# A two-block transformer kernel: FFN panel splits moved behind the tile work, keys copied by DMA, banks and table reads reordered

## The chip, the core and the metric

The kernel runs on one core of one Trainium2 chip. The metric is the time of one execution on the device, in microseconds. TensorE is PE (its weight loads are PEld), VectorE is DVE, ScalarE is ACT, GpSimd is POOL, and SyncE is SP, which issues nearly all DMAs.

## The reference

A sequence of 256 tokens, width 1024, fp32, runs through two blocks. Block 1 has two layers: a gated unit (gMLP) and then a convolutional FFN; differential attention with a relative bias and then a second such FFN. Block 2: a SwiGLU FFN, a mixer of latent attention (MLA) and block attention (MoBA) with positions, a second SwiGLU FFN, and a last norm.

```python
def conv_ffn(x, w_up, conv_w, conv_b, w_down):          # D_FF = 2816
    h = causal_dwconv(x @ w_up, conv_w, conv_b)
    g, u = h[..., :D_FF], h[..., D_FF:]
    return (jax.nn.gelu(g) * u) @ w_down
def swiglu(x, w_gate, w_up, w_down):
    return (jax.nn.silu(x @ w_gate) * (x @ w_up)) @ w_down
...
z = jax.nn.gelu(x @ w_in); u, v = z[..., :W], z[..., W:]   # gMLP
v = einsum('gpq,bnqgc->bnpgc', ws, layernorm(v)) + b_s
return (u * v) @ w_out
...
bias = rel_bias[t5_bucket(kpos - qpos)]                    # diff_attention, added to the scores
...
q, k = [q_nope, apply_rope(q_rope)], [k_nope, apply_rope(k_rope)]   # mla_attention
```

## The kernel before

All weights lie in HBM as 352 panels of 128x1024 fp32 (512 KB). Each goes the same way. SP loads panel n into `raw`, a ring of five buffers (`load(n)`, which waits until DVE has finished panel n-5). ACT copies it to `w_high` in the short format of TensorE (L441), and DVE subtracts to get `w_low` (L853); both are rings of eight. PE multiplies each product in three parts (high by high, high by low, low by high). Queues are written out by hand: each engine runs its list in order, and waits on semaphores. `upto(n)` on ACT and on DVE is a call that splits all panels up to n at this place of the list, so how far the splits run ahead is a matter of where these calls stand.

The stages by panel number: GMLP (24 panels), FFN0 (66), DIFF (32), FFN1 (66), FFN2 (66), MIX (32), FFN3 (66). In an FFN the hidden width is cut in 22 tiles f. Tiles 0 and 1 come from the first four panels of the stage (`first_four`, `first_two`, `turn_first`); for f from 2 on PE makes gate and up products (g, u: L1404 and L1408), and from f = 4 on also the down product (d) of tile f-4 (L1462). The last six down panels are in `tail`, which also begins the next stage. For a tile of a convolutional FFN the work goes: ACT copies the low product out (`lows_out`, L528), DVE adds it (`summed`, L957), ACT does the last tap (`last_tap`, L556), DVE the other taps (`first_taps`, L984), ACT the gelu (L562), DVE the product (`gated_up`, L993), ACT the high part (`hidden_high`, L532), DVE the low part (`hidden_low`, L966). Between them stand calls of `share(f, base, left)`, which spread the splits of the panels that have room in the ring. PE starts g of tile 4 only when `summed` of tile 2 is done, since both use one pair of PSUM banks, and d of tile f only after `hidden_low(f)`.

At a stage boundary b (`boundary(b)`) y is added to h, h is normed, and PE turns the parts (`turn_x`, L1470) and starts the value products (L1439 to L1445). In GMLP a product with ones spreads the first rms over partitions (`r0`), another gives row sums; both go to banks of Y, as do the eight u tiles (`tile_out`, L1389 to L1391). In MIX, `krt` holds the rotated shared key, which goes to all eight heads of `kT` (POOL, L426); `column_factors` on PE gives the factors of queries and keys, `CR` and `rkv`, and `cb_r` tells that both are read. The table `rel_rows` of the bias is written to HBM, and read back in eight DMAs `table_rows(a)` into `bias`, which POOL finishes (`bias_r`).

Of the kernel before, what the change touches and what calls it, by code (L numbers as in the profile page):

```python
# [91 lines left out]
def build_program(nc, io):  # L92
    with ExitStack() as ctx:
# [29 lines left out]
        CRs, rkvs = sb("cr", [P, T]), sb("rkv", [P, T])  # L123
# [3 lines left out]
        diag = sb("diag", [P, TT, P])  # L127
# [19 lines left out]
        lamrow = sb("lamrow", [P, 4, DIFF_D])  # L147
        posi = sb("posi", [P, T + TT], I32)
        posb = sb("posb", [P, 2, T + TT], I32)
# [8 lines left out]
        posf = w3[:, 0, 0:3 * (T + TT)].rearrange("p (a b) -> p a b", a=3)  # L158
        vg = big1[:].rearrange("p (t c) -> p t c", t=TT)
# [17 lines left out]
        CR, rkv = CRs[:], rkvs[:]  # L177
# [127 lines left out]
        def _(sp):  # L305
# [46 lines left out]
            for n in range(10, PANELS):  # L352
# [4 lines left out]
                if n == FFN0 + 2:  # L357
                    sp.wait_ge(vp_r, 2)
                    sp.wait_ge(rel_wr, 16)
                    sp.dma_start(lamrow[:].rearrange("p a b -> p (a b)"),  # L360
                                 io["lam"].to_broadcast([P, 4 * DIFF_D])).then_inc(lam_in, 16)
                if n >= FFN0 + 6 and (n - FFN0 - 6) % 4 == 0 and n < FFN0 + 6 + 32:
                    table_rows((n - FFN0 - 6) // 4)
# [9 lines left out]
        def _(pool):  # L373
# [30 lines left out]
            for q, c0, n in ((0, 0, P), (1, P, T)):  # L404
# [26 lines left out]
        def _(act):  # L431
# [88 lines left out]
            def share(f, base, left):  # L520

                seen = base + (FFN_AT["u", f] if f >= 2 else 4)
# [11 lines left out]
            def ffn(ph, base, with_conv):  # L534
                upto(base + 4)
                first_two(ph, base)
                if with_conv:
                    conv_ffn(ph, base)
                else:
                    swiglu_ffn(ph, base)  # L540
                preload(ACT.Sqrt)
                upto(base + 3 * NF + 1)

            def conv_ffn(ph, base):
# [19 lines left out]
                for f in range(NF):  # L564
# [4 lines left out]
                    if f < NF - 1:  # L569
                        share(f, base, 3)  # L570
# [192 lines left out]
            upto(DIFF + 34)  # L763
# [80 lines left out]
        def _(dve):  # L844
# [55 lines left out]
            def boundary(b):  # L900

                base = STARTS[b]
                if b in POST:
# [5 lines left out]
                    upto(base + (3 if b in (1, 3) else 2))  # L909
# [38 lines left out]
            def share(f, base, left):  # L948
                seen = base + (FFN_AT["u", f] if f >= 2 else 4)
                todo = min(seen + RING - (f < NF - 2), PANELS - 1) + 1 - made[0]  # L950
# [26 lines left out]
            def conv_ffn(ph, base):  # L977
# [18 lines left out]
                for f in range(NF):  # L996
# [5 lines left out]
                    if f < NF - 1:  # L1002
# [6 lines left out]
                upto(base + 3 * NF)  # L1009
# [82 lines left out]
            v.tensor_scalar(posb[:, 0, :], posi[:], 12, None, ALU.arith_shift_right)  # L1092
            link(v.tensor_scalar(posb[:, 1, :], posi[:], 4095, None, ALU.bitwise_and))
            v.tensor_copy(posf[:, 0, :], posi[:])
            v.tensor_copy(posf[:, 1:3, :], posb[:]).then_inc(pos_r, 1)
            upto(10)
            for t in range(TT):
# [5 lines left out]
                if t == 0:  # L1103
                    dve.wait_ge(r0_ps, 1)
                    v.tensor_copy(rkvs[:], Y[:, 2, 0:T]).then_inc(r0_r, 1)
# [6 lines left out]
            for k in range(KT):  # L1112
                r = Y[:, k // 4, (k % 4) * P:(k % 4 + 1) * P]
# [10 lines left out]
            U_BANK = (2, 0, 1, 3)  # L1124
# [130 lines left out]
            upto(DIFF + 34)  # L1255
# [40 lines left out]
            upto(B + 16)  # L1296
# [3 lines left out]
            dve.wait_ge(cb_r, 1)  # L1300
            weigh(8)
# [79 lines left out]
        def _(pe):  # L1381
# [235 lines left out]
            pe.wait_ge(ws_masked, 1)  # L1617
            for c in range(2):
                last = mm(Y[:, c, :], ones[:], wsT[:, half(c)], start=True, stop=True)
            last.then_inc(rowsum_r, 1)  # L1620
            pe.wait_ge(r0_r, 1)
            for k in range(KT):
                if k == 2:
                    pe.wait_ge(off_r, 1)
# [8 lines left out]
                tile_out(GMLP + 8 + k, Y[:, (2, 0, 1, 3)[k // 2], (k % 2) * T:(k % 2 + 1) * T])  # L1633
# [4 lines left out]
            pe.wait_ge(u_r, 3)  # L1638
# [192 lines left out]
            pe.wait_ge(kt_rot, 1)  # L1831
# [163 lines left out]
```

## Time and profile before

| | before |
|---|---|
| median of 3 runs | 1089.14 us (1087.27 to 1092.41) |
| the profiled execution, its own time | 1089.01 us |
| its span in the trace | 1087.2 us |
| PE busy | 97% of the span |
| DVE busy | 72% |
| ACT busy | 60% |
| mean granted TensorE clock | 0.997 of full speed |

The busy shares are means over all stages. The time is bounded by PE wherever PE has no idle time; the places where it has some, and who ended it, are what the views below are read for.

### The profile page before, as it was taken

How to read it: one execution, taken by the hardware profiler on the slowest of the kernel's cores; microseconds unless marked ns; L12 is line 12 of the kernel's file. 1: busy time of each engine (PE TensorE's matmuls, PEld its weight loads, DVE VectorE, ACT ScalarE, POOL GpSimd, SP SyncE). 2: the span in 40 equal slices, each digit the busy share in tenths (PEclk: the TensorE clock that was granted, in tenths of full speed). 3: DMA queues.
4: the chain of work that ended last, by engine and by line, in shares of the span. 5: the costliest groups of instructions: out<-in, count | busy, mean ns of one | idle time of the engine just before them, and what ended most of it. 6: DMA issues, size and time to landing. Idle time of an engine off the chain costs nothing.

```text
span 1087.2 us, 15597 instructions
## 1 busy us (share of the span) xinstructions
PE 1057.9 (97%) x5944; PEld 912.6 (84%) x5944; DVE 777.7 (72%) x1229; ACT 654.2 (60%) x1176; POOL 38.4 (4%) x39
## 2 busy tenths in 40 slices
PE   7999899999999999999999999999999999999997
PEld 5887788888799878888887888888898988888886
DVE  5887978887867889887787765566666857556554
ACT  6667656656657877665667654455555657455444
POOL 0830000000000000000000000000010000000000
PEclk9999999999999999999999999999999999999999
DMA  9764766555473347655662755656353625655651
GB/s 352 253 204 137 219 200 202 182 189 192 133 255 116 98 136 232 213 189 182 204 200 89 262 180 193 204 179 231 101 180 128 205 68 166 210 186 181 196 185 39
DMA packets 56250, 197.62 MB, mean 182 GB/s; under 512 B 6560, under 2 KB 8008, under 8 KB 56176
## 3 DMA queue, kind: packets, MB, share of 16 engines
q1 hardware_dynamic: 55920, 196.42, 55.1%
q8 instruction: 48, 0.79, 0.3%
q14 instruction: 26, 0.21, 0.1%
q0 software_dynamic: 112, 0.20, 0.1%
q10 hardware_dynamic: 144, 0.00, 0.0%
HBM read 195.35 MB, written 1.25 MB: 181 GB/s over the span
## 4 chain that ended last, share of the span: by engine, by line
PE 82%; DVE 8%; ACT 5%; DMA 3%; issue 2%; SPq 0%; ACTq 0%; DVEq 0%
PE G L1404 25%; PE Y L1462 23%; PE G L1408 13%; DVE w_low L853 3%; PE G L1389 3%; PE G L1390 3%; PE G L1391 3%; DMA raw<-in_panels 2%; PE G L1439 1%; ACT w_high L441 1%; DVE w L984 1%; PE G L1445 1%; PE G L1440 1%; PE Y L1457 1%; PE G L1587 1%
## 5 line engine op out<-in xcount | busy, mean ns | idle before, releaser
L853 DVE TENSOR_TENSOR w_low<-raw,w_high 128x1024 fp32r<-128x1024 f32 x352 | 425.5, 1228 | 44.8 <-ACT w_high L441 43.2
L441 ACT CAST w_high<-raw 128x1024 fp32r<-128x1024 f32 x352 | 363.5, 1046 | 16.0 <-DMA raw<-in_panels 14.4
L1404 PE MATMUL G<-x_parts,w_high 128*128 128x512 f32 x1280 | 321.0, 393 | 4.4 <-DVE w L957 4.4
L1404 PEld LDWEIGHTS G<-x_parts,w_high 128*128 128x128 f32 x1280 | 234.8, 189 | 49.9 <-DVE w L957 4.8
L528 ACT COPY big<-G 128x512 f32<-128x512 f32 x80 | 46.9, 586 | 237.7 <-PE G L1408 237.6
L1408 PEld LDWEIGHTS G<-x_parts,w_low 128*128 128x128 f32 x1280 | 175.2, 191 | 12.6
L1408 PE MATMUL G<-x_parts,w_low 128*128 128x256 f32 x1280 | 178.9, 283 | 0.0
L957 DVE TENSOR_TENSOR w<-G,big 128x512 f32<-128x512 f32 x80 | 55.3, 691 | 163.8 <-ACT big L528 163.6
L1462 PE MATMUL Y<-w_high,a_high 128*128 128x512 f32 x420 | 132.0, 395 | 2.6 <-DVE a_low L966 2.6
L1462 PE MATMUL Y<-w_high,a_low 128*128 128x512 f32 x420 | 130.0, 390 | 0.0
L1462 PE MATMUL Y<-w_low,a_high 128*128 128x512 f32 x420 | 129.7, 390 | 0.0
L1462 PEld LDWEIGHTS Y<-w_high,a_low 128*128 128x128 f32 x420 | 78.9, 188 | 17.3
L1462 PEld LDWEIGHTS Y<-w_low,a_high 128*128 128x128 f32 x420 | 78.9, 188 | 17.1
L1462 PEld LDWEIGHTS Y<-w_high,a_high 128*128 128x128 f32 x420 | 73.2, 189 | 13.4 <-DVE a_low L966 3.4
L984 DVE SCALAR_TENSOR_TENSOR w<-w,par 128x255 f32<-128x255 f32 (+1 forms) x160 | 70.2, 480 | 2.8 <-ACT w L556 1.4
L1389 PE MATMUL G<-x_parts,w_high 128*128 128x256 f32 x224 | 64.3, 287 | 0.0
L1390 PE MATMUL G<-x_parts,w_high 128*128 128x256 f32 x224 | 63.3, 283 | 0.0
L1391 PE MATMUL G<-x_parts,w_low 128*128 128x256 f32 x224 | 63.3, 283 | 0.0
L1439 PE MATMUL G<-w_high,x_parts 128*128 128x512 f32 x140 | 56.0, 400 | 1.7 <-DVE w_low L853 1.7
L1445 PE MATMUL G<-w_high,x_parts 128*128 128x512 f32 x140 | 54.7, 390 | 0.0
L1440 PE MATMUL G<-w_low,x_parts 128*128 128x512 f32 x140 | 54.5, 389 | 0.0
L556 ACT ACTIVATE w<-w,par 128x256 f32<-128x256 f32 x80 | 43.7, 594 | 6.0 <-DVE w L957 6.0
(247 smaller groups left out, 1186.0 us busy)
## 6 DMA issues: line engine op xcount, KB each, us to landing
raw<-in_panels SPq DMA_DIRECT2D x352, 512.0 KB, 4.3
gain_pre<-in_gains SPq DMA_DIRECT2D x7, 512.0 KB, 5.6
gain_post<-in_gains SPq DMA_DIRECT2D x4, 512.0 KB, 6.6
big<-in_xT SPq DMA_DIRECT2D x4, 256.0 KB, 7.4
h<-in_x SPq DMA_DIRECT2D x2, 512.0 KB, 8.9
big<-rel_rows SPq DMA_DIRECT2D x8, 128.0 KB, 5.2
out_y<-w SPq DMA_DIRECT2D x4, 256.0 KB, 2.2
big<-in_w_s SPq DMA_DIRECT2D x1, 512.0 KB, 10.0
```

The costliest lines, as they stand in the source:

```text
L441: s.copy(WH[:, n % RING, :], raw[:, n % RAWS, :]).then_inc(hi, 1)
L853: v.tensor_tensor(WL[:, n % RING, :], raw[:, n % RAWS, :], WH[:, n % RING, :].bitcast(F32), ALU.subtract).then_inc(lo, 1)
L984: last = v.scalar_tensor_tensor(out=wb[:, f % 2, m, T - n:T], in0=gate_of(f, m)[:, 0:n], scalar=par[:, c:c + 1], in1=wb[:, f % 2, m, T - n ...
L1389: mm(out, WH[:, j, c:c + w], xh, start=first, stop=False, skip_group_check=skip)
L1390: mm(out, WH[:, j, c:c + w], xl, start=False, stop=False, skip_group_check=skip)
L1391: return mm(out, WL[:, j, c:c + w], xh, start=False, stop=last, skip_group_check=skip)
L1404: mm(out, WH[:, n % RING, k * P:(k + 1) * P], X2[:, k, :, :], start=k == 0, stop=False, skip_group_check=True)
L1408: last = mm(out[:, 0:T], WL[:, n % RING, k * P:(k + 1) * P], X2[:, k, 0, :], start=False, stop=k == KT - 1, skip_group_check=True)
L1439: mm(out, xh, hic, start=k == 0, stop=False)
L1440: mm(out, xh, loc, start=False, stop=False)
L1445: last = mm(out, xl, hic, start=False, stop=k == KT - 1)
L1462: end = mm(Y[:, 2 * t + c, :], x, w[:, j, half(c)], start=start, stop=stop)
```

## The change

Nothing is computed otherwise. There are these parts.

1. In a convolutional FFN the calls of `share` for tiles 0 and 1 are fewer and later (`seen` counts 2 + f panels instead of 4, and the first of a tile's calls falls away), DVE's splits keep one panel less ahead at the end, and the splits of the next stage's first panels come after the last tile's work instead of between it. In swiglu the new `seen` holds too, and ACT's table load for the next stage comes after its splits.
2. At boundary 3 one split moves from before the first `y_square` and `y_gained` to after it, and the split of panel base+3 moves to where boundary 2 has it.
3. The eight `table_rows` are issued from load FFN0+18 on instead of FFN0+6.
4. The copy of `krt` to eight heads is a DMA on SP (ahead of load MIX+24) instead of a POOL instruction; `CR` overwrites `facq`, and CR and rkv are made before the splits of MIX+15 and MIX+16.
5. In GMLP the spread rms uses bank 1, the row sums banks 2 and 3, and the u tiles go through banks 0, 1, 2, 3 in order; PE's waits for `r0_r` and `off_r` stand ahead of tiles 2 and 4 instead of 0 and 2.
6. Six small buffers are laid over others; the count of raw buffers stays five.

```diff
@@ sync @@
-                if n >= FFN0 + 6 and (n - FFN0 - 6) % 4 == 0 and n < FFN0 + 6 + 32:
-                    table_rows((n - FFN0 - 6) // 4)
+                if FFN0 + 18 <= n < FFN0 + 50 and (n - FFN0 - 18) % 4 == 0:
+                    table_rows((n - FFN0 - 18) // 4)
+                if n == MIX + 24:
+                    sp.wait_ge(kr_r, 1)
+                    sp.dma_start(kT[ROT:P, :, :], krt[ROT:P, :].unsqueeze(1).to_broadcast([P - ROT, HEADS, T]))\
+                        .then_inc(kt_rot, 16)
@@ gpsimd @@
-            pool.wait_ge(kr_r, 1)
-            g.tensor_copy(kT[ROT:P, :, :], krt[ROT:P, :].unsqueeze(1).to_broadcast([P - ROT, HEADS, T]))\
-                .then_inc(kt_rot, 1)
@@ scalar and vector, boundary @@
-                    upto(base + (3 if b in (1, 3) else 2))
+                    upto(base + (3 if b == 1 else 2))
@@ scalar and vector, share @@
-                seen = base + (FFN_AT["u", f] if f >= 2 else 4)
+                seen = base + (FFN_AT["u", f] if f >= 2 else 2 + f)
@@ vector, share @@
-                todo = min(seen + RING - (f < NF - 2), PANELS - 1) + 1 - made[0]
+                todo = min(seen + RING - 1, PANELS - 1) + 1 - made[0]
@@ scalar, ffn @@
+                upto(base + 3 * NF + 1)
                 preload(ACT.Sqrt)
-                upto(base + 3 * NF + 1)
@@ scalar and vector, conv_ffn @@
-                    if f < NF - 1:
+                    if f == NF - 1:
+                        upto(base + 3 * NF - 1)
+                    elif f >= 2:
                         share(f, base, 3)
...
-                upto(base + 3 * NF)
@@ scalar, ahead of boundary 3 @@
-            upto(DIFF + 34)
@@ vector, ahead of boundary 3 @@
-            upto(DIFF + 34)
+            upto(DIFF + 33)
@@ vector, MIX @@
-            upto(B + 16)
             dve.wait_ge(cbc, 1)
             v.tensor_tensor(CR, facq[:], PB[:, 0:T], ALU.mult)
             v.tensor_copy(rkv[0:64, :], PB[0:64, T:2 * T]).then_inc(cb_r, 1)
             dve.wait_ge(cb_r, 1)
+            upto(B + 16)
@@ tensor, GMLP @@
-                last = mm(Y[:, 2, t * P:(t + 1) * P], ones[:], diag[:, t, :], start=True, stop=True)
+                last = mm(Y[:, 1, t * P:(t + 1) * P], ones[:], diag[:, t, :], start=True, stop=True)
...
-                last = mm(Y[:, c, :], ones[:], wsT[:, half(c)], start=True, stop=True)
+                last = mm(Y[:, 2 + c, :], ones[:], wsT[:, half(c)], start=True, stop=True)
...
-            pe.wait_ge(r0_r, 1)
             for k in range(KT):
                 if k == 2:
+                    pe.wait_ge(r0_r, 1)
+                if k == 4:
                     pe.wait_ge(off_r, 1)
...
-                tile_out(GMLP + 8 + k, Y[:, (2, 0, 1, 3)[k // 2], (k % 2) * T:(k % 2 + 1) * T])
+                tile_out(GMLP + 8 + k, Y[:, k // 2, (k % 2) * T:(k % 2 + 1) * T])
...
-            pe.wait_ge(u_r, 3)
+            pe.wait_ge(u_r, 2)
```

First place: ACT's list at the start of FFN0, from the split behind the second `first_two` copy to `lows_out` of tile 2. CAST w_high is a split, ACTIVATE w<-Y,par a last tap of tile 0 or 1, ACTIVATE w<-w the gelu, CAST a_high `hidden_high`, COPY big<-G `lows_out`. Before:

```order
L441 CAST w_high<-raw 128x1024 [waits landed2,panels_used]
L441 CAST w_high<-raw 128x1024 [waits landed3,panels_used]
L441 CAST w_high<-raw 128x1024 [waits landed4,panels_used]
L556 ACTIVATE w<-Y,par 128x256 [waits first_two_turned]
L556 ACTIVATE w<-Y,par 128x256
L441 CAST w_high<-raw 128x1024 [waits landed0,panels_used]
L441 CAST w_high<-raw 128x1024 [waits landed1,panels_used]
L562 ACTIVATE w<-w 128x256 [waits taps_r]
L556 ACTIVATE w<-Y,par 128x256 [waits first_two_turned]
L556 ACTIVATE w<-Y,par 128x256
L532 CAST a_high<-w 128x256 [waits product]
L528 COPY big<-G 128x512 [waits panels_used]
```

After, over the same work:

```order
L442 CAST w_high<-raw 128x1024 [waits landed2,panels_used]
L557 ACTIVATE w<-Y,par 128x256 [waits first_two_turned]
L557 ACTIVATE w<-Y,par 128x256
L442 CAST w_high<-raw 128x1024 [waits landed3,panels_used]
L442 CAST w_high<-raw 128x1024 [waits landed4,panels_used]
L563 ACTIVATE w<-w 128x256 [waits taps_r]
L557 ACTIVATE w<-Y,par 128x256 [waits first_two_turned]
L557 ACTIVATE w<-Y,par 128x256
L442 CAST w_high<-raw 128x1024 [waits landed0,panels_used]
L533 CAST a_high<-w 128x256 [waits product]
L529 COPY big<-G 128x512 [waits panels_used]
L563 ACTIVATE w<-w 128x256 [waits taps_r]
```

Three splits stood ahead of the first last tap and two more ahead of the first gelu; now one stands ahead of that tap, two more ahead of the gelu, and another ahead of `hidden_high`.

Second place: DVE's list for tiles 20 and 21 of FFN0. The first row is the split call of tile 20; then come `first_taps`, `hidden_low`, splits, `summed`, `gated_up`, and tile 21. Before:

```order
L853 TENSOR_TENSOR w_low<-raw,w_high 128x1024 [waits high_split] x2
...
L853 TENSOR_TENSOR w_low<-raw,w_high 128x1024 [waits high_split] x2
L957 TENSOR_TENSOR w<-G,big 128x2x256 [waits lows_r]
L993 TENSOR_TENSOR w<-w 128x256 [waits gated,taps_r,summed]
L984 SCALAR_TENSOR_TENSOR w<-w,par 128x255 [waits tap2]
L984 SCALAR_TENSOR_TENSOR w<-w,par 128x255
L984 SCALAR_TENSOR_TENSOR w<-w,par 128x254 [waits vector_chain]
L984 SCALAR_TENSOR_TENSOR w<-w,par 128x254
L966 TENSOR_TENSOR a_low<-w,a_high 128x256 [waits hid_high]
L853 TENSOR_TENSOR w_low<-raw,w_high 128x1024 [waits high_split]
L993 TENSOR_TENSOR w<-w 128x256 [waits gated,taps_r]
L966 TENSOR_TENSOR a_low<-w,a_high 128x256 [waits hid_high]
```

After:

```order
L855 TENSOR_TENSOR w_low<-raw,w_high 128x1024 [waits high_split]
...
L855 TENSOR_TENSOR w_low<-raw,w_high 128x1024 [waits high_split] x2
L959 TENSOR_TENSOR w<-G,big 128x2x256 [waits lows_r]
L995 TENSOR_TENSOR w<-w 128x256 [waits gated,taps_r,summed]
L855 TENSOR_TENSOR w_low<-raw,w_high 128x1024 [waits high_split]
L986 SCALAR_TENSOR_TENSOR w<-w,par 128x255 [waits tap2]
L986 SCALAR_TENSOR_TENSOR w<-w,par 128x255
L986 SCALAR_TENSOR_TENSOR w<-w,par 128x254 [waits vector_chain]
L986 SCALAR_TENSOR_TENSOR w<-w,par 128x254
L968 TENSOR_TENSOR a_low<-w,a_high 128x256 [waits hid_high]
L995 TENSOR_TENSOR w<-w 128x256 [waits gated,taps_r]
L968 TENSOR_TENSOR a_low<-w,a_high 128x256 [waits hid_high]
```

One split moved from tile 20 to between `gated_up(20)` and the taps of tile 21, and the split that stood ahead of `gated_up(21)` moved behind the last `hidden_low`.

Third place: DVE's list in MIX, from the rotated key (krt) to the split ahead of the next scores. Before:

```order
L1294 TENSOR_TENSOR krt<-krt,cosk 64x256
L1295 TENSOR_TENSOR krt<-krt,rot 64x256 [waits vector_chain]
L853 TENSOR_TENSOR w_low<-raw,w_high 128x1024 [waits high_split] x2
L1298 TENSOR_TENSOR cr<-facq,G 128x256 [waits cbc]
L1299 COPY rkv<-G 64x256
L1047 RECIPROCAL rs<-sm 128x4 [waits exp_r,cb_r]
L853 TENSOR_TENSOR w_low<-raw,w_high 128x1024 [waits high_split]
L1035 SCALAR_TENSOR_TENSOR w<-dist,Y 128x384 [waits scores_r]
```

After:

```order
L1297 TENSOR_TENSOR krt<-krt,cosk 64x256
L1298 TENSOR_TENSOR krt<-krt,rot 64x256 [waits vector_chain]
L1300 TENSOR_TENSOR facq<-facq,G 128x256 [waits cbc]
L1301 COPY rkv<-G 64x256
L855 TENSOR_TENSOR w_low<-raw,w_high 128x1024 [waits high_split,cb_r]
L855 TENSOR_TENSOR w_low<-raw,w_high 128x1024 [waits high_split]
L1050 RECIPROCAL rs<-sm 128x4 [waits exp_r]
L855 TENSOR_TENSOR w_low<-raw,w_high 128x1024 [waits high_split]
```

The two splits moved from ahead of the factors to behind them.

## Rows read from the trace of the kernel before

**Rows 1.** Page, part 1: busy us (share of the span) and instructions of an engine

```profile
PE 1057.9 (97%) x5944; PEld 912.6 (84%) x5944; DVE 777.7 (72%) x1229; ACT 654.2 (60%) x1176; POOL 38.4 (4%) x39
```

**Rows 2.** Waits of PE: total us, times, longest us

```profile
PE G L1404 <- DVE w L957: 4.4, 2, 2.7
PE Y L1470 <- DVE w L892: 4.2, 9, 1.1
PE Y L1462 <- DVE a_low L966: 2.6, 2, 1.3
PE G L1439 <- DVE w_low L853: 1.7, 2, 0.9
...
PE Y L1389 <- DVE rkv L1105: 0.7, 1, 0.7
...
PE Y L1389 <- DVE big L1114: 0.3, 1, 0.3
```

**Rows 3.** Timeline of PE, start of FFN 0: start us, us, instruction, idle before

```profile
101.85 0.60 PE L1539 MATMUL Y<-cst,big 128*128 128x128 f32 x4
...
105.09 2.00 PE L1404 MATMUL G<-x_parts,w_high 128*128 128x512 f32 x8
...
107.88 2.00 PE L1404 MATMUL G<-x_parts,w_high 128*128 128x512 f32 x8
...
113.57 3.27 PE L1404 MATMUL G<-x_parts,w_high 128*128 128x512 f32 x8 [2.74 <-DVE w L957]
...
118.03 2.02 PE L1404 MATMUL G<-x_parts,w_high 128*128 128x512 f32 x8
```

**Rows 4.** Windows, one microsecond after that idle: busy of engines, PEclk

```profile
115.00:116.00 1.00, 1.00 (x4) 0.81 (x3) 0.96 (x4) 0.74 (x2) 0.00 (x0) 0.50 0.07 16
```

**Rows 5.** Timeline of ACT, start of FFN 0

```profile
102.89 1.05 ACT L441 CAST w_high<-raw 128x1024 fp32r<-128x1024 f32 x1 [1.75 <-DMA raw<-in_panels]
...
105.46 1.02 ACT L556 ACTIVATE w<-Y,par 128x256 f32<-128x256 f32 x2
...
111.23 0.58 ACT L528 COPY big<-G 128x512 f32<-128x512 f32 x1
```

**Rows 6.** Timeline of DVE, start of FFN 0

```profile
112.83 0.69 DVE L957 TENSOR_TENSOR w<-G,big 128x512 f32<-128x512 f32 x1
```

**Rows 7.** Timeline of DVE, last two tiles of FFN 0

```profile
259.94 2.35 DVE L853 TENSOR_TENSOR w_low<-raw,w_high 128x1024 fp32r<-128x1024 f32 x2
...
264.05 1.79 DVE L984 SCALAR_TENSOR_TENSOR w<-w,par 128x255 f32<-128x255 f32 x4 [0.71 <-ACT w L556]
```

**Rows 8.** Timeline of PE, end of FFN 0 and the next boundary

```profile
266.24 0.73 PE L1462 MATMUL Y<-w_high,a_high 128*128 128x512 f32 x2 [1.28 <-DVE a_low L966]
...
276.64 0.83 PE L1470 MATMUL Y<-cst,w 128*128 128x128 f32 x4 [0.59 <-DVE w L892]
```

**Rows 9.** Timeline of DVE, start of the latent attention

```profile
813.49 2.47 DVE L853 TENSOR_TENSOR w_low<-raw,w_high 128x1024 fp32r<-128x1024 f32 x1 [0.36 <-ACT w_high L441]
815.99 0.42 DVE L1298 TENSOR_TENSOR cr<-facq,G 128x256 f32<-128x256 f32 x1
```

**Rows 10.** Timeline of POOL, same stretch

```profile
811.93 2.94 POOL L426 COPY big<-krt 64x2048 f32<-64x2048 f32 x1 [642.34 <-DVE krt L1295]
```

**Rows 11.** Timeline of ACT, same stretch

```profile
815.55 0.37 ACT L617 COPY qk<-G 128x256 f32<-128x256 f32 x1
```

**Rows 12.** Timeline of PE, the matmuls that make the factors, and PE behind them

```profile
811.30 1.06 PE L1740 MATMUL G<-big,ones 128*128 128x128 f32 x8
...
816.79 0.55 PE L1587 MATMUL G<-cst,w 128*128 128x128 f32 x3 [1.56 <-DVE rkv L1299]
```

**Rows 13.** Page, part 6: DMA issues, KB each, median us to landing

```profile
raw<-in_panels SPq DMA_DIRECT2D x352, 512.0 KB, 4.3
...
big<-rel_rows SPq DMA_DIRECT2D x8, 128.0 KB, 5.2
```

**Rows 14.** Timeline of PE, first use of the rotated keys

```profile
852.12 0.39 PE L1572 MATMUL Y<-big 128*128 128x128 f32 x2
```

More of the change, by code:

```diff
@@ L122, in build_program @@
         krt, rot = sb("krt", [P, T]), sb("rot", [P, T])
-        CRs, rkvs = sb("cr", [P, T]), sb("rkv", [P, T])
+        rkvs = sb("rkv", [P, T])
         par = sb("par", [P, N_PAR])
@@ L126, in build_program @@
         ones = sb("ones", [P, P])
-        diag = sb("diag", [P, TT, P])
+        diag = big2[:, 0:TT * P].rearrange("p (t q) -> p t q", t=TT)
         rtc = sb("rtc", [P, 4])
@@ L146, in build_program @@
         subg = sb("subg", [P, 1])
-        lamrow = sb("lamrow", [P, 4, DIFF_D])
-        posi = sb("posi", [P, T + TT], I32)
-        posb = sb("posb", [P, 2, T + TT], I32)
+        lamrow = rkvs[:].rearrange("p (a b) -> p a b", a=4)
+        posi = dist[:, 0:T + TT].bitcast(I32)
         Y = ps("Y", [P, 4, 512])
@@ L158, in build_program @@
         posf = w3[:, 0, 0:3 * (T + TT)].rearrange("p (a b) -> p a b", a=3)
+        posb = w3[:, 0, 3 * (T + TT):5 * (T + TT)].rearrange("p (a b) -> p a b", a=2).bitcast(I32)
         vg = big1[:].rearrange("p (t c) -> p t c", t=TT)
@@ L176, in build_program @@
         csq = w3[:, 1, 0:5 * T].rearrange("p (k t) -> p k t", k=5)
-        CR, rkv = CRs[:], rkvs[:]
+        CR, rkv = facq[:], rkvs[:]
         csum = big2[:, 0:2 * T].rearrange("p (a t) -> p a t", a=2)
@@ L908, in boundary @@
                     half_mean(b, 0)
-                    upto(base + (3 if b in (1, 3) else 2))
+                    upto(base + (3 if b == 1 else 2))
                     x_normed(b, 0)
@@ L948, in share @@
             def share(f, base, left):
-                seen = base + (FFN_AT["u", f] if f >= 2 else 4)
-                todo = min(seen + RING - (f < NF - 2), PANELS - 1) + 1 - made[0]
+                seen = base + (FFN_AT["u", f] if f >= 2 else 2 + f)
+                todo = min(seen + RING - 1, PANELS - 1) + 1 - made[0]
                 upto(made[0] - 1 + -(-todo // left))
@@ L1001, in conv_ffn @@
                         gated_up(f - 1)
-                    if f < NF - 1:
+                    if f == NF - 1:
+                        upto(base + 3 * NF - 1)
+                    elif f >= 2:
                         share(f, base, 3)
@@ L1091, in _ @@
             dve.wait_ge(pos_in, 32)
[L1092 to L1095, printed above, removed]
+            v.tensor_scalar(posb[:, 0, :], posi, 12, None, ALU.arith_shift_right)
+            link(v.tensor_scalar(posb[:, 1, :], posi, 4095, None, ALU.bitwise_and))
+            v.tensor_copy(posf[:, 0, :], posi)
+            v.tensor_copy(posf[:, 1:3, :], posb).then_inc(pos_r, 1)
             upto(10)
@@ L1104, in _ @@
                     dve.wait_ge(r0_ps, 1)
-                    v.tensor_copy(rkvs[:], Y[:, 2, 0:T]).then_inc(r0_r, 1)
+                    v.tensor_copy(rkvs[:], Y[:, 1, 0:T]).then_inc(r0_r, 1)
             link(last)
@@ L1112, in _ @@
             for k in range(KT):
-                r = Y[:, k // 4, (k % 4) * P:(k % 4 + 1) * P]
+                r = Y[:, 2 + k // 4, (k % 4) * P:(k % 4 + 1) * P]
                 last = v.scalar_tensor_tensor(out=off[:, k, :], in0=r, scalar=par[:, C_LNB + k:C_LNB + k + 1],
@@ L1123, in _ @@
             last.then_inc(vhat_r, 1)
-            U_BANK = (2, 0, 1, 3)
+            U_BANK = (0, 1, 2, 3)
             def scale_u(k):
@@ L1830, in _ @@
             pe.wait_ge(mk_r, 1)
-            pe.wait_ge(kt_rot, 1)
+            pe.wait_ge(kt_rot, 16)
             scores(12)
```

3 lines of the change are left out of this document (2 added, 1 removed).

## The prediction

> **What bounds the kernel now.** I read the page's first part, then the waits of PE, then the timelines around each wait. PE is busy for 1057.9 of 1087.2 us [rows 1], so 29.3 us is all that any reordering can give back, unless PE also runs faster somewhere. The waits of PE [rows 2] say where to look, since a wait by a part of the kernel costs nothing unless it shows there. The steady middle of each FFN has none, although DVE and ACT wait often in it: there PE alone sets the pace. What the change can reach is: 2.7 us (the longest of the two L1404 waits) at the start of FFN0 and 4.4 - 2.7 = 1.7 at that of FFN1; two of 1.3 (L1462 on a_low) at the ends of FFN0 and FFN1; 1.56 for rkv in MIX [rows 12]; 0.7 + 0.3 in GMLP; and part of the nine waits of L1470 at boundaries (4.2 in total, longest 1.1, which is boundary 3; one of 0.59 is in [rows 8]). The 1.7 of L1439 is a wait of 0.85 for a split at each of boundaries 2 and 4.
>
> One more cost is not idle time. Eight L1404 matmuls and their L1408 take 107.88 - 105.09 = 2.79 us, but behind the 2.74 us wait the same work takes 118.03 - 113.57 = 4.46 [rows 3]; the granted clock there is 0.50, so 1.2 GHz instead of 2.4 [rows 4]. That is 1.67 us more.
>
> **The start of FFN0.** g of tile 4 waits for `summed(2)`. That is late since DVE starts it at 112.83 [rows 6], and before it wants `lows_out(2)`, which ACT reaches at 111.23 [rows 5]. ACT was late from the first last tap on: 105.46, behind a split that itself waited 1.75 us for its panel, and another. I move the lists as front shows. PE's turn of the first tiles ends near 101.85 + 0.60 = 102.45 [rows 3], so the tap runs at 102.5 to 103.5; two splits of 1.0 follow to 105.5; DVE has done its taps (1.8) at 105.3; gelu and the next last tap end at 106.8, a split at 107.8, `hidden_high` at 108.1, and `lows_out` at 108.7. On DVE the taps of tile 1 end at 108.6, `hidden_low` at 108.9, one split (1.2, half of the x2 row in [rows 7]) at 110.1, `summed(2)` at 110.8. PE finishes u of tile 3 at 113.57 - 2.74 = 110.83. So the wait goes, with nothing in hand: I take 2.7 gained, with 2.2 as the low end. What is late next is the split that was put off. It is one panel; g and u of tile 4 need panels that are split by then, the next `summed` is needed 8.3 us later (three panels of 2.75 to 2.8) and DVE's list up to it is 0.65 + 0.35 + 1.2 + 1.8 + 0.35 + 1.2 = 5.6 us, so the cover holds and grows with each tile. With the wait gone I also count the 1.67 of the half clock. The table rows, 128 KB each with 5.2 us to landing [rows 13], leave this stretch, and I count nothing for it, since the list above already works with the landings of before.
>
> The Trainium skill (TensorE: Matmul & The Clock Gate, "What's actually happening") has the clock follow how busy PE has been of late, and says that the point of change varies with the phase of a window that runs free. By that rule the half clock can come or stay away from run to run, so against a median up to 1.7 us of my sum may be no gain; the trace has one such drop behind a 2.74 us wait, and none behind the 1.7 us wait of FFN1.
>
> **The start of FFN1** has the same lists with a shorter wait, 1.7. The same steps end `summed(2)` before PE is done with tile 3: 1.7.
>
> **FFN2 and FFN3** have no such wait before, and get fewer early splits: 0. What covers it is that DVE has no taps there.
>
> **The ends of FFN0 and FFN1.** PE waits 1.28 for `hidden_low(20)` [rows 8]. Before, DVE ran two splits, taps, two splits (259.94 + 2.35), `summed(21)` behind them at 262.2, and the taps of tile 21 at 264.05, held by ACT's last tap [rows 7]. In the new list one split less stands ahead of `summed(21)`: it starts 1.15 us earlier, at 261.1; `gated_up(20)` ends at 262.2, and the moved split fills what was a wait for ACT, to 263.4. Taps 1.7, so `hidden_low(20)` ends at 265.45 instead of 266.1. PE wants it at 266.24 - 1.28 = 264.96 or a little before. So only about half goes: 0.65 each (from 0 if ACT's tap does not come earlier, to 1.28). Behind it the next stage's splits no longer stand between y and the norm alone: ACT's table load comes later, but DVE starts `y_gained` about 0.75 us nearer to PE's end of y. That is more than the 0.59 us wait for `turn_x` [rows 8], and I take 0.6 at each of boundaries 2 and 4. Their wait of 0.85 for the split of base+3 depends on a chain that starts at y of the second half and stays. Sum of both ends: 2 x (0.65 + 0.6) = 2.5.
>
> **Boundary 3.** The wait of 1.1 goes, since DVE has one split (1.15) less ahead of `y_gained`, and some 0.8 of short waits behind it go too. But the split of base+3 now stands where boundaries 2 and 4 have it, where it costs 0.85, and here PE has no half of a last down product (1.4 us, half of twelve matmuls) in between; the chain begins 0.4 earlier. The new wait is 0.85 + 1.4 - 0.4, about 1.7, bounded by 0.85 and 2.2. Net 1.9 - 1.6 = 0.3, from -0.4 to 1.0.
>
> **MIX.** The factors come at 815.99, behind a split that took 2.47 us instead of 1.2 while POOL copied the key for 2.94 [rows 9, 10]. In the new list they follow the rotated key and the factors' matmuls (811.30 + 1.06 = 812.4), and are there at 813.2, before PE asks (816.79 - 1.56 = 815.2) [rows 12]. PE then turns, and waits for ACT's copy of queries and keys, whose last piece runs at 815.55 to 815.92 [rows 11]. So the scores start at 816.0 instead of 817.26: 1.3 gained, not 1.6. The two splits end later relative to the factors but at 815.6 in all, since the slow one is short again; their panels are wanted from 819 on.
>
> The new DMA is 512 KB in 1 KB pieces. SP comes to it behind load MIX+23, which waits for the split of MIX+18. That one follows the factors by rkv 0.8, a split 1.2, the scores' sum and maxima 2.3, and itself 1.2 with short steps between: near 821.7, when the key has long been rotated, and nothing queues behind a wait. PE wants the keys at 852.12 [rows 14]. Landing is bounded by 4.3 us (a panel of the same bytes) and 4 x 5.2 = 21 (table rows, 128 KB in the same pieces) [rows 13]; both lie inside 30. I take 0.
>
> **GMLP.** The two waits, 0.7 and 0.3, are for reads of banks that PE would overwrite. With free banks first each read has two tiles (5.7 us) more of cover, against waits of 0.7 and less: 1.0 gained. DVE's list is unchanged.
>
> The later table rows end about 12 panels x 2.8 = 34 us later, still some 90 us ahead of the attention: 0.
>
> **The sum**: 2.7 + 1.7 + 1.7 + 2.5 + 0.3 + 1.3 + 1.0 = 11.2 us. From the profiled execution's own 1089.0 (the median of the runs is 1089.1) that is 1077.8 us.
>
> **The rivals.**
> *The split lists leave a rest.* DVE's list at the starts of FFN0 and FFN1 has no slack; a landing or a semaphore a microsecond late leaves 1 us at each, the half clock stays, and the FFN ends give nothing: 11.2 - 2 - 1.7 - 1.3 = 6.2, so 1082.8. For it speaks that the first 0.1 us decide; against it that DMA there is relieved.
> *No change to speak of.* The put-off splits turn into waits of PE for w_low in the first tiles of all four FFNs. Each panel late costs 1.2; two for each of four stages take 9.6 of the 11.2: 1087.4. Against it speak the 8.3 against 5.6 us for each tile.
> *Slower.* The key DMA holds up PE at L1572. Its place in the queue is fixed, so it must take over 30 us to cost anything, and over 30 + 11.2 + 5.4 = 47 for a time that is 0.5% above before; at 47 us the time is 1094.5. The nearest rows allow 21 at most. The Trainium skill (DMA: Bandwidth & Descriptors, "Why small descriptors are slow (HBM only)") says that transfers inside SBUF are spared the cost of small pieces; by it the lower bound is the nearer one, and this case has nearly no chance.
> *The change does more*: if ACT's chain lets all of both 1.28 go and boundary 3 keeps its 1.0, the sum is 13.2: 1075.8.
>
> **The numbers.** Forecast 0.62, a rest left 0.20, more 0.08, no change 0.07, slower 0.03. The forecast's own range is 1076 to 1080. To hold 8 in 10 I reach to the rest left on one side and past "more" on the other: 1075.0 to 1083.5. A difference under 0.5% (5.4 us) can't be told from none here, as the three runs span 5.1 us. Faster by over 0.5% takes the forecast, "more", and most of the rest: 0.87; within 0.5%: 0.10; slower: 0.03.
>
> **What the profile after would show.** Waits of PE: no L1404 wait at the starts of FFN0 and FFN1 above 0.3 us, and no 0.5 clock inside; about 0.6 left on a_low at two FFN ends; no wait for rkv or for spread or offset in GMLP; L1439 waits for w_low up from 1.7 to 3 to 3.5 us with a third one at boundary 3; PE busy share near 98%. The key DMA lands within 21 us, and the split beside it in MIX takes 1.2. I am wrong if L1404 still waits over 1 us in a convolutional FFN, if new waits for w_low stand inside an FFN, or if L1572 waits for the DMA.

## The result, and the profile after

The changed kernel takes 1076.04 us (median of 4, 1075.06 to 1076.59) against 1089.99 of the kernel before (4 runs, 1087.27 to 1092.41): a ratio of 0.9872, interval 0.9846 to 0.9898. The forecast was 1077.8 with a range of 1075.0 to 1083.5, so the direction and the range held, and the time lies 1.8 us under the forecast.

The profiled execution of the changed kernel has an own time of 1076.43 us, a span of 1074.6 and a granted clock of 0.998. The page's first part answers to [rows 1]:

```profile
PE 1054.8 (98%) x5944; PEld 911.8 (85%) x5944; DVE 776.3 (72%) x1229; ACT 654.5 (61%) x1176; POOL 36.4 (3%) x38
```

PE has the same 5944 matmuls. In the chain that ended last PE's share rose from 82% to 93% and DVE's fell from 8% to 4%. The waits of PE after the change (total us, times, longest us), for [rows 2]:

```profile
PE G L1422 <- ACT w_high L442: 7.2, 1, 7.2
PE G L1442 <- DVE w_low L855: 3.0, 3, 1.4
PE Y L1473 <- DVE w L894: 1.2, 4, 0.4
PE Y L1465 <- DVE a_low L968: 1.1, 2, 0.5
PE G L1473 <- DVE w L894: 0.4, 2, 0.2
PE Y L1575 <- ACT qk L620: 0.4, 1, 0.4
```

Gone are the rows for `summed` (L1404 before, L1407 now), for `rkv` in the latent attention, and both of the gated unit. The first row is the wait at the program's start, for the first panel; it was 6.9 before and isn't touched. The w_low row has grown from two waits to three, the a_low row has fallen from 2.6 to 1.1, and the row of the turns (L1470 before, L1473 now) from nine waits of 4.2 to four of 1.2. The timeline of PE after the change (start us, us, instruction, idle before) shows the start of FFN 0, the end of FFN 0 and the three w_low waits:

```profile
104.18 2.00 PE L1407 MATMUL G<-x_parts,w_high 128*128 128x512 f32 x8
...
106.97 2.00 PE L1407 MATMUL G<-x_parts,w_high 128*128 128x512 f32 x8
...
109.77 1.61 PE L1407 MATMUL G<-x_parts,w_high 128*128 128x512 f32 x6
...
260.07 0.73 PE L1465 MATMUL Y<-w_high,a_high 128*128 128x512 f32 x2 [0.54 <-DVE a_low L968]
...
277.14 0.50 PE L1442 MATMUL G<-w_high,x_parts 128*128 128x512 f32 x1 [0.85 <-DVE w_low L855]
...
390.17 0.50 PE L1442 MATMUL G<-w_high,x_parts 128*128 128x512 f32 x1 [1.37 <-DVE w_low L855]
...
577.71 0.50 PE L1442 MATMUL G<-w_high,x_parts 128*128 128x512 f32 x1 [0.80 <-DVE w_low L855]
```

Tiles 2, 3 and 4 of FFN 0 now begin 2.79 and 2.80 us apart, with no idle at 109.77. DVE's side of it, for [rows 6], is that `summed(2)` starts 24.84 us behind boundary 1's turn (108.98 - 84.14) and not 27.79 (112.83 - 85.04), so 2.95 us earlier, with one split ahead of it, as the prediction's list had it:

```profile
107.51 0.42 DVE L968 TENSOR_TENSOR a_low<-w,a_high 128x256 fp32r<-128x256 f32 x1
107.84 1.22 DVE L855 TENSOR_TENSOR w_low<-raw,w_high 128x1024 fp32r<-128x1024 f32 x1
108.98 0.69 DVE L959 TENSOR_TENSOR w<-G,big 128x512 f32<-128x512 f32 x1
```

It ends at 109.67, 0.1 us before PE asks: the cover is as thin as the prediction said.

**Where the time came from.** I take the two traces apart at PE rows that both have. From boundary 1's turn (85.04 before, 84.14 after) to the last boundary's turn (893.88, 881.42) the kernel before takes 808.84 us and the changed one 797.28. This stretch, called B below, leaves the start of the program out, which moves by over a microsecond between executions. It ends ahead of FFN 3, so that and the last norm lie outside it too. "The column" is from here on the idle time that a row of the timeline has in brackets. The experiments are compared by it, since a single time can't tell 0.5 us.

| stretch | before, us | after, us | gained | predicted |
|---|---|---|---|---|
| boundary 1 to g of tile 4 in FFN 0 | 28.53 | 25.63 | 2.90 | 2.7 |
| from there to the a_low wait | 152.67 | 150.30 | 2.37 | 1.7 + 0.65 |
| to boundary 2's w_low wait | 18.02 | 17.07 | 0.95 | 0.6 |
| to g of tile 4 in FFN 1 (boundary 3) | 135.45 | 133.10 | 2.35 | 0.3 + 1.7 |
| from there to the a_low wait | 151.11 | 150.31 | 0.80 | 0.65 |
| to boundary 4's w_low wait | 18.07 | 17.16 | 0.91 | 0.6 |
| to the turn at 777.06 / 765.89 | 188.17 | 188.18 | 0.0 | 0 |
| to the last turn (latent attention) | 116.82 | 115.53 | 1.29 | 1.3 |
| B | 808.84 | 797.28 | 11.56 | 10.2 |

The gated unit lies ahead of B and gave 0.90 in this pair (predicted 1.0). Behind B, FFN 3 and the last norm took 193.3 us before and 193.2 after. Together that is the 12.6 us between the spans.

No experiment below undoes the new lists at the ends of FFN 0 and FFN 1 by themselves. That rows two (beyond the clock), three, five and six of the table come from them is an argument by what is left: in the seven kernels that undo another part each, the start lists among them, the third stretch stays between 17.06 and 17.08 us and the sixth between 17.12 and 17.16, and a second execution of the kernel before has 18.03 and 18.07 again.

### The profile page after: what moved, and what is told of

The parts are those of the page before. It is cut to its first block, busy times and chain, and to the rows that moved or that the text cites. A ratio compares the mean times of both kernels' runs of the same rounds, so it can differ in the third digit from the quotient of the medians.

```text
span 1074.6 us, 15598 instructions
## 1 busy us (share of the span) xinstructions
PE 1054.8 (98%) x5944; PEld 911.8 (85%) x5944; DVE 776.3 (72%) x1229; ACT 654.5 (61%) x1176; POOL 36.4 (3%) x38
## 4 chain that ended last, share of the span: by engine, by line
PE 93%; DVE 4%; ACT 2%; issue 1%; DMA 0%; SPq 0%; ACTq 0%
PE G L1407 27%; PE Y L1465 25%; PE G L1411 14%; PE G L1392 3%; PE G L1393 3%; PE G L1394 3%; PE G L1442 2%; PE G L1443 2%; PE G L1448 2%; PE Y L1460 1%; DVE w_low L855 1%; PE Y L1393 1%; PE Y L1392 1%; PE Y L1394 1%; PE G L1590 1%; PE Y L1473 1%
## 5 line engine op out<-in xcount | busy, mean ns | idle before, releaser
L1407 PE MATMUL G<-x_parts,w_high 128*128 128x512 f32 x1280 | 319.6, 392 | 0.0
L1407 PEld LDWEIGHTS G<-x_parts,w_high 128*128 128x128 f32 x1280 | 234.1, 188 | 44.7
```

Source lines behind the costliest of these rows:

```text
L1407: mm(out, WH[:, n % RING, k * P:(k + 1) * P], X2[:, k, :, :], start=k == 0, stop=False, skip_group_check=True)
```

## The experiments

Each kernel is the changed kernel with one edit, but for two that start from the kernel before, and say so. The expectations count from the rel-bias matmul (L1612, before L1609) to the last turn. That stretch turned out to hold a wait whose end does not follow PE (see the gated unit), so I read the results by B, and give the other where the two differ.

**The old lists at the starts of FFN 0 and FFN 1.**

```diff
-                seen = base + (FFN_AT["u", f] if f >= 2 else 2 + f)
+                seen = base + (FFN_AT["u", f] if f >= 2 else 4)
-                    elif f >= 2:
+                    else:
                         share(f, base, 3)
```

(on both engines)

> The changed kernel with only the split calls of tiles 0 and 1 as they were. Lists theory: PE waits for summed(2) again, 2.5 to 2.8 us in FFN0 and 1.6 to 1.8 in FFN1, span 1074.6 + 4.4 = 1079.0, and 1080.7 if the half clock comes back behind the longer wait. Rival (the start of FFN0 was helped by the table rows leaving it): at most 1 us of wait in FFN0, span under 1077.5.

Measured: 1080.15 us (median of 4), ratio 0.9904 (0.9884 to 0.9923) to before. B is 801.23, 3.95 more than in the changed kernel: 1.93 at FFN 0 and 1.91 at FFN 1. The rest is in FFN 2, whose lists this edit sets back as well: from boundary 4 to the latent attention it takes 188.36 us and not 188.18. The waits of PE and two windows behind the first wait (the third number from the right is the granted clock):

```profile
PE G L1407 <- DVE w L959: 3.4, 2, 1.7
```
```profile
111.00:112.00 1.00, 0.67 (x3) 0.59 (x4) 0.97 (x3) 1.00 (x2) 0.00 (x0) 1.00 0.53 209
112.00:113.00 1.00, 1.00 (x6) 0.82 (x5) 1.00 (x2) 1.00 (x4) 0.00 (x0) 1.00 0.10 33
```

So the lists are what moves `summed(2)`, in both stages. But here the lists alone make a wait of 1.71 in FFN 0, not before's 2.74 (I had expected 2.5 to 2.8), and no clock of 0.5 comes behind it.

**The table rows back at FFN0 + 6.**

```diff
-                if FFN0 + 18 <= n < FFN0 + 50 and (n - FFN0 - 18) % 4 == 0:
+                if FFN0 + 6 <= n < FFN0 + 38 and (n - FFN0 - 6) % 4 == 0:
```

> The changed kernel with the eight table reads at their old loads. Lists theory: landings of before were already in the worked list, which has 0.1 us in hand, so 0 to 0.5 us of wait at the start of FFN0, span 1074.6 to 1075.1. Rival (table rows made the wait): 1 to 4 us more.

Measured: 1075.55 us, B 797.20, and no new wait. With the new lists the place of these rows is worth nothing.

**The kernel before with the table rows late** (the same two lines the other way round, in the kernel before).

> The kernel before with one edit, the table rows issued 12 panels later. Theory from the runs so far (lists alone give a wait of 1.7, table rows early on top of the old lists make it 2.74): the wait of tile 4's g in FFN0 is 1.7, the half clock behind it stays away, and the time from the rel-bias matmul to the last turn is 2.7 us less than before's 873.55 (1.0 from the wait, 1.7 from the clock). Rival (the 2.74 comes from something else in the old order, such as the unit's banks): the wait stays above 2.4. If the clock dips behind 1.7 as well, only 1.0 is gained.

Measured: 1091.44 us, B 811.52 (876.83 from the rel-bias matmul). The wait in FFN 0 is 2.00, and from boundary 1's turn to g of tile 4 it takes 27.82 us against 28.53 in the profile of before, 28.27 in the repeat below and 27.51 with the old lists in the changed kernel. So the rows' place was worth 0.45 to 0.71 us of that wait, not the 1.0 I expected, by one execution against two that differ by 0.26 themselves. The other 0.3 I did not take apart. The clock did worse than expected: three drops to the lower level (1.2 GHz), where before's profile has one. The windows:

```profile
113.00:114.00 1.00, 1.00 (x3) 0.77 (x3) 1.00 (x2) 1.00 (x3) 0.00 (x0) 0.51 0.28 111
420.00:421.00 1.00, 1.00 (x5) 0.75 (x4) 1.00 (x3) 1.00 (x3) 0.00 (x0) 0.61 0.01 4
...
820.00:821.00 1.00, 1.00 (x6) 1.00 (x6) 0.97 (x3) 1.00 (x2) 0.00 (x0) 0.50 0.91 119
```

They stand behind waits of 2.00, 1.85 and 1.56 us.

**The kernel before once more, for its trace.**

> The kernel before once more, for its trace alone. If the half clock behind the 2.74 us wait belongs to the wait, it stands here too, and from the rel-bias matmul to the last turn the trace shows 873.5 within 0.3. If it comes and goes with the execution, it is absent here, and the same stretch takes 871.9.

Measured: 1089.91 us, B 810.15 (875.30 from the rel-bias matmul). Neither reading fits whole: the drop at FFN 0's wait (2.46 here) stands again, and a second one has come behind FFN 1's, which had none before:

```profile
419.14 1.17 PE L1404 MATMUL G<-x_parts,w_high 128*128 128x512 f32 x3 [1.96 <-DVE w L957]
```
```profile
113.00:114.00 1.00, 1.00 (x3) 0.81 (x4) 1.00 (x2) 1.00 (x3) 0.00 (x0) 0.50 0.19 74
420.00:421.00 1.00, 1.00 (x4) 0.71 (x4) 1.00 (x3) 1.00 (x4) 0.00 (x0) 0.50 0.09 37
```

The size of a drop can be read six times, as the same stretch with and without one. From FFN's tile 4 to the a_low wait it is 152.67 - 151.11 = 1.56 in before's own two stages, and 1.54 and 1.55 in FFN 1 of these two kernels; in the latent attention it is 78.65 - 77.09 = 1.56. FFN 0 of the kernel with late rows gives 1.55 against the same 151.11. FFN 0 of this one gives less, 152.48 - 151.11 = 1.37. There the drop had begun before the wait was over (PE goes on at 112.90), so that PE had no work in a part of it:

```profile
112.00:113.00 1.00, 0.10 (x1) 0.10 (x1) 0.96 (x3) 1.00 (x2) 0.00 (x0) 0.76 0.88 348
```

Three traces in the old order have 1, 2 and 3 drops, and B less 1.56 for each is 807.28, 807.03 and 806.84: the rest of the program is the same within half a microsecond.

**Boundary 3 as before.**

```diff
-                    upto(base + (3 if b == 1 else 2))
+                    upto(base + (3 if b in (1, 3) else 2))
...
-            upto(DIFF + 33)
+            upto(DIFF + 34)
```

(the first line on both engines, the second on DVE; ACT gets its `upto(DIFF + 34)` back too)

> The changed kernel with the lists around boundary 3 as before (one more split ahead of the norm on each engine, the split of base+3 ahead of it). My step said: the old waits there (1.07 and some 0.8 of short ones) against a new w_low wait; the profile after showed the new wait as 1.37. Theory: the 1.37 is gone, 1.07, 0.23, 0.39 and 0.23 are back, and from the rel-bias matmul to the last turn the program takes 0.3 to 0.8 us more than the changed kernel. Rival (the short waits are modelling dust and cost nothing): it takes 0.3 us less, since 1.07 is smaller than 1.37.

Measured: 1075.65 us, B 797.80, 0.52 more than the changed kernel. The timeline of PE:

```profile
382.86 0.84 PE L1474 MATMUL Y<-cst,w 128*128 128x128 f32 x4 [1.05 <-DVE w L895]
383.92 0.66 PE L1474 MATMUL G<-cst,w 128*128 128x128 f32 x4 [0.22 <-DVE w L895]
...
390.45 0.83 PE L1474 MATMUL Y<-cst,w 128*128 128x128 f32 x4 [0.39 <-DVE w L895]
391.51 0.66 PE L1474 MATMUL Y<-cst,w 128*128 128x128 f32 x4 [0.23 <-DVE w L895]
```

The exchange at boundary 3 is real, and gains about half a microsecond. Of the 2.35 in the table's fourth row that leaves 1.8 for the start of FFN 1, near the 1.91 of the first experiment.

**The last split behind `hidden_low(20)`.**

```diff
-                    if f == NF - 1:
-                        upto(base + 3 * NF - 1)
-                    elif f >= 2:
+                    if 2 <= f < NF - 1:
                         share(f, base, 3)
                     first_taps(f)
                     if f:
                         hidden_low(ph, f - 1)
+                    if f == NF - 1:
+                        upto(base + 3 * NF - 1)
```

> The changed kernel, with DVE's half of the last panels' splits behind hidden_low(20) at the ends of FFN0 and FFN1 instead of ahead of the last taps. Theory (DVE's list ahead of hidden_low(20) makes the a_low wait): both 0.54 waits go, hidden_low(20) ends up to 1.2 us earlier, and the whole takes 0.5 to 1.6 us less; the late split costs no new wait, since PE wants that panel only behind it. Rival (ACT's last tap ends last there): the waits stay at about 0.5 and the time is the same. Second rival: the late split pushes y_gained back and the boundary takes the gain again, so a w_low wait at boundaries 2 and 4 grows by as much.

Measured: 1076.13 us, B 797.29: nothing gained. The a_low waits fall from 0.54 to 0.20 and 0.19, so DVE's list did cause most of them. PE reaches them 0.32 and 0.38 us earlier, and by the next w_low wait it has given 0.48 and 0.43 back. That is the second rival, but by another road than it said: the w_low waits stay at 0.85 and 0.84. What is late is DVE: its last split ahead of the norm starts 177.84 us behind boundary 1's turn (261.74 - 83.90), and in the changed kernel 177.34 (261.48 - 84.14). Those 0.50 are what PE gives back.

The timeline of DVE in that kernel, where the split stood before the taps:

```profile
257.32 1.79 DVE L986 SCALAR_TENSOR_TENSOR w<-w,par 128x255 f32<-128x255 f32 x4 [0.70 <-ACT w L557]
259.03 0.42 DVE L968 TENSOR_TENSOR a_low<-w,a_high 128x256 fp32r<-128x256 f32 x1
259.37 1.22 DVE L855 TENSOR_TENSOR w_low<-raw,w_high 128x1024 fp32r<-128x1024 f32 x1
```

Without the split DVE waits 0.70 for ACT's last tap. The split had filled that wait.

**The split of base + 3 ahead of the second half's norm** (`upto(base + 3)` on DVE before `y_gained(b, 1, 0)`).

> The changed kernel, with DVE's split of panel base+3 moved ahead of y_gained of the second half at the boundaries. Theory (the chain behind the second half's y makes the split of base+3 late): the three w_low waits of 0.80 to 1.37 go, and in their place x_low or h of the second half is at most 1.2 us later, under PE's first products; 1 to 3 us less. Rival (the split is only exchanged for the second half's chain): the w_low waits go and a wait of the same size for w or for turn_x of the second half comes; time within 0.5 us of the changed kernel, or above it.

Measured: 1076.36 us, B 797.27: nothing gained. All three w_low waits are gone, and PE waits for the turn of the second half instead (0.38, 0.76 and 0.36, each with a further 0.22 or 0.23 behind it). The exchange rival is right. One chain on DVE feeds both, and whichever part stands last in it is waited for.

**Both together.**

> The two edits together (last split behind hidden_low(20), split of base+3 ahead of the second half's norm), as a candidate that beats both kernels. If both theories hold the gains add: 1071.5 to 1074.5 us against 1076 for the changed kernel. If the exchange rival holds for the boundary, 1075 to 1077. If the late last split and the early base+3 split now stand on either side of one norm and delay it, above 1077.

Measured: 1075.37 us (median of 4, 1075.21 to 1075.71), ratio 0.9868 (0.9852 to 0.9885), B 797.48. The intervals of the ratios lie over one another and B is 0.2 longer, so this is no better version. I found none that beats the changed kernel.

**The latent attention: the factors behind the split, as before.**

```diff
+            upto(B + 16)
             dve.wait_ge(cbc, 1)
...
-            upto(B + 16)
```

> The changed kernel with the two splits of MIX ahead of the factors again, key still copied by DMA. Order theory (my step): PE waits for rkv again, 1.3 us more, span 1075.9. Rival (the wait came from the POOL copy that made a split 2.47 us long): splits are 1.2 us each, the factors are ready 0.3 us behind PE's question at most, span 1074.6 to 1074.9.

Measured: 1075.38 us, B 797.33; from the turn at 765 to the last one 115.66 us, against 115.53 in the changed kernel. A wait of 0.31 for `rkv` takes the place of the 0.41 for `qk`.

**GpSimd copies the key, as before** (the transfer taken out, the copy back in, PE waits for that).

> The changed kernel with the key copied by POOL again, factors still ahead of the splits. Order theory: the slow split (2.4 us) stands behind the factors and is hidden, span 1074.6 to 1074.9. Rival (the POOL copy was what cost): some of the 1.3 us comes back, span 1075.4 or more.

Measured: 1075.81 us, B 797.02; the same stretch takes 115.46.

**Both at once.**

> The changed kernel with both parts of the MIX change undone (GpSimd copies the key, the factors stand behind the split). Theory: together they are what gave 1.3 us, though either alone did not matter (0.46 and -0.26 from the rel-bias matmul to the last turn): the slow split of 2.4 us and the rkv wait of about 1.5 come back, and the program takes 1.2 to 1.6 us more than the changed kernel. Rival (the gain in MIX came from elsewhere, such as the transfers ahead of it): the wait is under 0.8.

Measured: 1077.15 us; the same stretch takes 116.76, 1.23 more than in the changed kernel (1.09 from the rel-bias matmul). The timelines of DVE and of PE in this kernel, and then of DVE in the one with the copy alone:

```profile
800.27 1.23 DVE L855 TENSOR_TENSOR w_low<-raw,w_high 128x1024 fp32r<-128x1024 f32 x1
801.86 2.47 DVE L855 TENSOR_TENSOR w_low<-raw,w_high 128x1024 fp32r<-128x1024 f32 x1 [0.36 <-ACT w_high L442]
804.36 0.42 DVE L1301 TENSOR_TENSOR facq<-facq,G 128x256 f32<-128x256 f32 x1
```
```profile
805.16 0.55 PE L1590 MATMUL G<-cst,w 128*128 128x128 f32 x3 [1.57 <-DVE rkv L1302]
```

```profile
800.75 0.42 DVE L1300 TENSOR_TENSOR facq<-facq,G 128x256 f32<-128x256 f32 x1 [0.53 <-PE G L1745]
801.09 0.41 DVE L1301 COPY rkv<-G 64x256 f32<-64x256 f32 x1
801.53 2.86 DVE L855 TENSOR_TENSOR w_low<-raw,w_high 128x1024 fp32r<-128x1024 f32 x2
```

The two parts are not a sum of two gains. Either takes most of the wait away: without the copy the second split is 1.22 us and `rkv` comes only 0.31 behind PE's question. With the factors first PE finds them there, and the split beside the copy is less slow (1.73 of the 2.86 for the two), with nobody waiting for it. Undoing one costs nothing that can be told, undoing both costs all of it.

**The gated unit's banks in the old order.**

```diff
-                last = mm(Y[:, 1, t * P:(t + 1) * P], ones[:], diag[:, t, :], start=True, stop=True)
+                last = mm(Y[:, 2, t * P:(t + 1) * P], ones[:], diag[:, t, :], start=True, stop=True)
...
+            pe.wait_ge(r0_r, 1)
             for k in range(KT):
                 if k == 2:
-                    pe.wait_ge(r0_r, 1)
-                if k == 4:
                     pe.wait_ge(off_r, 1)
```

(and with it the row sums, the u tiles and DVE's reads of all three in their old banks)

> The changed kernel with the order of banks in the gated unit as before. The working counted 1.0 for its two waits (0.70 and 0.33 in the idle column); the traces of before and after differ by 1.57 between the landmarks there. Theory (the idle column, counted from the modelled end of the matmul before, understates what a wait costs): 1.4 to 1.7 us more than the changed kernel from the rel-bias matmul to the last turn, with 0.70 and 0.33 in the column. Rival (the extra half microsecond came from another part, such as the diagonal's new place): 1.0 more.

Measured: 1076.93 us, B 797.26, and from the rel-bias matmul (L1612, at 20.28) to boundary 1's turn (84.71) 64.43 us. The changed kernel takes 63.15, and so do eight of the other variants within 0.01. The ninth, with the factors behind the split, takes 63.56; 0.32 of that is at one down product of the gated unit, behind a wait of 0.16 for which the trace names no releaser, and I did not find its cause. The wait in the trace, and the same place in the changed kernel:

```profile
32.47 1.88 PE L1622 MATMUL Y<-big,ones 128*128 128x512 f32 x4
35.12 0.39 PE L1392 MATMUL Y<-x_parts,w_high 128*128 128x256 f32 x1 [0.77 <-DVE rkv L1108]
```

```profile
33.18 1.88 PE L1623 MATMUL Y<-big,ones 128*128 128x512 f32 x4
34.50 0.68 PE L1392 MATMUL Y<-x_parts,w_high 128*128 128x256 f32 x1
```

The column says 0.77, and 64.43 - 63.15 = 1.28 is lost. That lies between the two readings (1.4 to 1.7, and 1.0), but for a single wait in the column, not for 1.03 in two: the theory's point holds, its size was for two waits. The idle counts from 32.47 + 1.88 = 34.35, the modelled end of the four. But where nothing holds PE up, the next matmul starts 1.32 us after the four's start and not 1.88. The 0.56 between is part of the cost and not in the column. The old order shows it three more times: 1.03 in the column (0.70 and 0.33) against 1.56 lost in the profile of before, 1.63 against 2.16 in the kernel with late table rows, and 1.48 against 2.00 in the repeat. The difference is 0.51 to 0.53 each time.

These four also say why the gain by the clock on the wall is smaller. The wait ends when DVE has read the bank into `rkv`. It starts that read at 34.58 to 34.66 us whenever PE came, and PE goes on at 35.03 to 35.12. In the old order an early PE only waits longer. So the gated unit is worth 1.28 to 2.16 by PE's own progress, and 0.90 in the pair of profiles, where the changed kernel's PE had started 0.66 late.

## Why the prediction was right, point by point

**The start of FFN 0**: right in mechanism and, at 2.90 for 2.7, in size. The column's 2.74 leaves out 0.16, and it does so at other waits too: 1.87 us were lost for 1.71 with the old lists, and 1.73 for 1.57 at `rkv` in the kernel with both parts of MIX undone. The step "I count nothing for it" on the table rows was right of the sum and wrong as a reading: their place was 0.45 to 0.71 us of the old wait, and the new lists cover it either way.

**The half clock**: 1.67 was counted, and a drop cost 1.56 in five readings of six. It is not one for each execution, though. In the three traces in the old order I count six drops; in the eleven traces of the changed kernel and its variants there is none inside the program. The mean clock of before's runs fits in the main (0.998 at 1088.28 us and 0.993 at 1092.16), but only three of them have a trace here. That before's median (1089.99) lies above its profiled execution (1089.01) is most likely this. It would be 0.98 of the 1.37 us by which the medians (13.95 apart) differ more than the profiled executions (12.58 apart); the other 0.39 is that the changed kernel's profiled execution was slower than its median. The Trainium skill (TensorE: Matmul & The Clock Gate, "What's actually happening") says that the point of change varies with a window that runs free. The traces agree as far as they go, since the same program dropped once and twice; but where I drew from it that the gain might be smaller against a median, it was larger.

**The start of FFN 1**: 1.7 predicted, 1.8 to 1.9 measured.

**The ends of FFN 0 and FFN 1**: mis-sized by a little. I wrote that "only about half goes: 0.65 each"; it was 0.80 (0.74 in the column, 1.28 to 0.54). At boundaries 2 and 4 I took 0.6 each, and 0.95 and 0.91 were gained. That I took from the idle column of [rows 8]: this is the largest mis-sized term (0.66 for both). The rows show where the rest sits. Before, the turn begins 10.40 us behind the a_low row (276.64 - 266.24) and the next down product 0.59 behind the turn; after it is 9.66 and 0.39:

```profile
277.23 0.48 PE L1457 MATMUL Y<-w_high,a_high 128*128 128x512 f32 x1
```
```profile
269.73 0.63 PE L1473 MATMUL Y<-cst,w 128*128 128x128 f32 x4
270.12 0.48 PE L1460 MATMUL Y<-w_high,a_high 128*128 128x512 f32 x1
```

So the turn's first matmul stood for 0.74 us more, of which the column has 0.59, and its four matmuls took another 0.20 that the column has nowhere.

**Boundary 3**: "about 1.7" for the new wait, 1.37 measured, and 0.3 net against 0.52.

**The latent attention**: 1.3 predicted, 1.29 measured, and PE does then wait for ACT's `qk` (0.41). The prediction puts it down to the order and counts 0 for the key's transfer. The step rests on two causes, the copy and the order, either of which would have done. The key's transfer (512 KB) took 6.0 us to landing, against bounds of 4.3 and 21, and nobody waited for it. The panels issued just before and just behind it took 4.1 and 6.5. The Trainium skill (DMA: Bandwidth & Descriptors, "Why small descriptors are slow (HBM only)") spares transfers inside SBUF the cost of small pieces. That 6.0 lies between the two panels agrees, but no run moves the same pieces from HBM.

**The gated unit**: right at 1.0 for the wrong reason. The columns' 1.0 understates what was lost there by 0.5; that PE's start varies took it back in the pair of profiles. That the two nearly cancel is luck.

**No change elsewhere** (FFN 2, FFN 3, the later table rows) held: the stretch from boundary 4 to the latent attention took 188.17 and 188.18, and the one behind B, with FFN 3, 193.3 and 193.2.

Of the rivals, "a rest left" did not come, though by 0.1 us. "The change does more" came near in its time (1075.8), but not in its mechanism: the a_low waits kept 0.54, and boundary 3 gave 0.5 and not 1.0.

## What to carry over

Price a wait by the distance between two starts, with and without it, and not by the idle column: behind the gated unit's four wide matmuls the column left out 0.5 us each time here, and at the other waits taken apart 0.15 to 0.16. Undo a change by parts and together: two parts may each remove the same wait. And a wait in a chain that feeds several consumers moves when its order is changed; two reorderings here took 3.0 and 0.7 us of waits out of the list and gained nothing.

## What the runs showed of the hardware

A drop of TensorE's clock to 1.2 GHz cost 1.54 to 1.56 us where PE had work all through it (five readings), and 1.37 where it began inside the wait. It came with waits of 1.56 to 2.74 us, not with each: of PE's waits of 1.85 and more (the one at the program's start aside) all five had one, of seven between 1.56 and 1.73 one had. That is a count and no threshold.

A DVE split of 1024 columns takes 1.22 us. With GpSimd's copy of the key running it took 2.47 in the kernel with both parts undone and 1.73 in the one with the copy alone, where the same place of the list takes 1.22 without the copy. The slow split ends 1.08 us behind the copy's end both times (804.33 and 803.25; 803.25 and 802.17). The first split in the kernel with both parts undone took 1.23 all the same: it had started 0.03 us ahead of the copy, and there the copy took 2.95 and not 1.89. All this fits that the one that starts second stands until the first is through. No run tests that alone, and spans on GpSimd are rough:

```profile
800.30 2.95 POOL L426 COPY big<-krt 64x2048 f32<-64x2048 f32 x1 [602.09 <-DVE krt L1298]
```
```profile
800.28 1.89 POOL L426 COPY big<-krt 64x2048 f32<-64x2048 f32 x1 [602.07 <-DVE krt L1298]
```
